# Four modulation halves summed partly by TensorE, their biases added in VectorE's step, and the scores of two heads issued together

## The chip, the cores and the metric

The kernel runs on one core of a Trainium2 chip. The metric is the device time of one execution in microseconds (us), the median of several. The core has five engines that work side by side and wait for one another by semaphores: TensorE (PE: matrix products; PEld is its weight load), VectorE (DVE), ScalarE (ACT), GpSimd (POOL) and SyncE (SP), which issues most of the transfers. Two memories matter here: SBUF, which holds operands, and PSUM, whose eight banks receive the products of TensorE.

## The reference, cut to what matters

One transformer block on a sequence of 512 tokens with 1024 features, all in fp32:

```python
cs = jax.nn.silu(c)
mod = cs @ w_ada + b_ada                       # 1024 -> 6 * 1024
sh1, sc1, g1, sh2, sc2, g2 = split(mod, 6)
h = rmsnorm(x, norm1_g) * (1 + sc1) + sh1
x = x + g1 * mixer(h, ...)                     # 16 heads of three kinds
h = rmsnorm(x, norm2_g) * (1 + sc2) + sh2
x = x + g2 * peer_ffn(h, ...)                  # 8 routed heads over 16384 experts
out = rmsnorm(x, final_g)
```

The mixer projects h by w_in (2560 columns) and has 4 heads of kind A (differential attention: two maps each, over 32 features), 6 of kind B (block attention, which at this length is causal attention over 64 features) and 6 of kind C (sliding window of 128 tokens with a sink, 64 features, two key heads shared by three query heads each). Every head has an ALiBi slope of its own.

## The kernel before, in words

**Start.** SP issues the loads of x, of the first biases, of the first three halves of w_ada (128 partitions x 8 x 512, 2 MB each), then tiles of w_in (w_raw, 0.5 MB each) and the fourth half (lines 825 to 835). `ADA_HALVES` numbers twelve halves of 512 modulation columns; halves 0 to 3 are scale and shift of the first norm. VectorE makes silu(c) and the small lambda and sink values (L1326 to L1338), waiting for ScalarE's exponential in between (L1036); ScalarE squares x (L1039) and takes the root (L1041); VectorE scales x by it (L1345), and TensorE transposes x into the banks (`x_columns`, L416).

**A modulation half** (`mod_half`) is eight VectorE steps over 128x512: L1358 multiplies the first block of w_ada with its silu column, L1360 adds the seven others. The accumulator mod_acc has two places, so half n waits until half n-2 has been used (`half_used`). For halves 0 to 3 TensorE sums over the partitions with one-column products, four per half into one PSUM bank (L427), each followed by a one-row product that adds the bias (L431). `a1_col` and `sh1_col` come out of that bank (L1383, L1385). For halves 4 to 11, `mod_row` on TensorE makes a row on all partitions: one product with ones (L442), one with a single row that adds the bias (L443), and VectorE copies it out (L1373, L1376).

**First normed input.** For each of eight blocks k, ScalarE writes h1_hi (L1071, rounded), VectorE writes h1 (L1390) and subtracts to h1_lo (L1393). `first_two` then projects the first two tiles of w_in with three products per block (L456, L457 and L462); the second of its banks, G, is the one from which the last block of x was read. w_in itself is split in the same way: ScalarE makes w_in_hi (L1048), GpSimd w_in_lo (L956).

**Attention.** It is a list of 64 jobs written out in order, one head on one tile of 128 queries each: kind C for the four query tiles, then A, then B. Iteration J of the loop on TensorE issues, in this order, the scores of job J+2 (L519), pieces of the projections still missing (L475 to L477, L495 to L497), a `mod_row` in some, the transposes of the probabilities of job J (L532), and the product with the values of job J-1 (L552). Score maps alternate between two banks, S0 and S1. VectorE's `soft_in` (L1414) reads a bank, adds the slope times distance, and gives the minimum; ScalarE takes the exponential (L1091) and copies the transposed probabilities (L1099). VectorE's iteration also holds two steps of a modulation half (jobs 0 to 29). In kind B and after it, TensorE transposes the finished output tiles (L563), multiplies by w_out (L578) and transposes the second normed input (L591); VectorE adds the residual (L1482, L1485, L1491) and divides the outputs (`group_out`, L1459). Line L1155 is a root on ScalarE between exponentials, each with a table load.

**The rest,** from about 385 us on, is the routed part: query and key scores, top-16 searches, gates by one-hot products, and a loop over 128 chunks of experts (L672 to L674 and L723), with gathered rows for the first token tile.

The order around the change is the program's own: each engine's list of instructions, the semaphores between them, and SP's single queue. Rows of a head in the array are set by its partitions:

```python
maps = [(h // 2, 2 + h // 2, 64 * (h % 2) + 32 * m, 32) for m in range(2)]     # kind A
[(4 + h // 2, 7 + h // 2, 64 * (h % 2), 64)]                                   # kind B
[(10 + h % CG, 13, 64 * kv, 64)]                                               # kind C, kv = h // CG
```

Of the kernel before, what the change touches and what calls it, by code (L numbers as in the profile page):

```python
# [21 lines left out]
RING = 6  # L22
AHEAD = 8
# [11 lines left out]

def head_plan():


    heads = []
    for h in range(NA):  # L40
        maps = [(h // 2, 2 + h // 2, 64 * (h % 2) + 32 * m, 32) for m in range(2)]
        heads.append(("A", maps, 32 ** -0.5, SLOPES[NCH + h], 256 + h * HD, h * HD, h, h))
    for h in range(NB):
        heads.append(("B", [(4 + h // 2, 7 + h // 2, 64 * (h % 2), 64)], 64 ** -0.5, SLOPES[NCH + NA + h],
                      512 + h * HD if h < 4 else (h - 4) * HD, 256 + h * HD, h, NA + h))
    for h in range(NCH):
        kv = h // CG
        heads.append(("C", [(10 + h % CG, 13, 64 * kv, 64)], 64 ** -0.5, SLOPES[h], 128 + kv * HD,
                      640 + h * HD, h, NA + NB + h))
    return heads  # L50
# [43 lines left out]
def peer_block_kernel(nc, x, c_col, norm1_col, w_ada, b_ada, w_in, w_out, lam_vecs, subln_row, sinks_row,  # L94
# [4 lines left out]
    with ctx:  # L99
# [90 lines left out]
        n1_col = sb("n1_col", [P, KD])  # L190
        a1_col = sb("a1_col", [P, KD])
        sh1_col = sb("sh1_col", [P, KD])
# [3 lines left out]
        subln = sb("subln", [P, HD])  # L196
        sinks = sb("sinks", [P, NCH])
# [37 lines left out]
        s_b, s_n2 = sem("first_biases_loaded"), sem("norm2_loaded")  # L235
        s_ada = [sem(f"ada_loaded{n}") for n in range(4)]
# [127 lines left out]

        def pv_count(J):

            return J + 1 - sum(last <= J for last in LAST)
# [17 lines left out]
        def _(pe):  # L385
# [36 lines left out]
            pe.wait_ge(s_b, 16)  # L422
            for n in range(4):
                pe.wait_ge(s_accd, n + 1)
                for m in range(4):
                    at = n * 4 + m
                    pe.matmul(mcols[:, at:at + 1], mod_acc[:, n % 2, m * P:m * P + P], ones[:, 0:1],  # L427
                              start=True, stop=False)
                    s, b = ADA_HALVES[n]
                    row = s * D + b * 512 + m * P  # L430
                    mm = pe.matmul(mcols[:, at:at + 1], b_first[0:1, row:row + P], ones[0:1, 0:1],  # L431
                                   start=False, stop=True)
                mm.then_inc(full["G"] if n == 3 else s_modu, 1)
            x_columns(KD - 1)

            def mod_row(n):

                b = side["next"]
                ps = take(b, ("row", n))
                pe.wait_ge(s_accd, n + 1)  # L440
                pe.wait_ge(s_bh[n % 3], 16 * ((n - 4) // 3 + 1))
# [69 lines left out]
            def scores(J):  # L511
                i, j = JOBS[J]
                kt = key_tiles(i, j)
                for m, (qt, kk, part, rows) in enumerate(plan[j][1]):
                    s = FIRST_MAP[J] + m
                    ps = take(f"S{s % 2}", ("s", s))
                    for n in NEEDS.get(J, ()):
                        emptied(("qk", n))
                    pe.matmul(ps[:, 0:len(kt) * P], qkT[part:part + rows, qt, i * P:i * P + P],  # L519
                              qkT[part:part + rows, kk, kt[0] * P:(kt[-1] + 1) * P],  # L520
                              start=True, stop=True).then_inc(full[f"S{s % 2}"], 1)
# [277 lines left out]
        def _(sp):  # L799
            def ada(n):  # L800
                s, b = ADA_HALVES[n]
                at = s * D + b * 512
                if n < 4:
                    sp.dma_start(ada_first[n][:, :, :], w_ada[:, at:at + 512].rearrange("(k p) c -> p k c", p=P))\
                      .then_inc(s_ada[n], 16)
                    return
                if n == 4:
                    sp.wait_ge(s_accd, 1)
                elif n == 5:
                    taken(sp, ("xT", KD - 1))  # L810
# [15 lines left out]
            sp.dma_start(b_first[0:1, :], b_ada[0:1, 0:2 * D]).then_inc(s_b, 16)  # L826
            for n in range(3):
                ada(n)
            win(0)
            ada(3)  # L830
# [103 lines left out]
        def _(pool):  # L934
            pool.memset(ident[:, :], 0.0).then_inc(s_const, 1)
# [90 lines left out]
        def _(act):  # L1026
            act.dma_start(c_in[:, :], c_col).then_inc(s_c, 16)
            act.dma_start(n1_col[:, :], norm1_col).then_inc(s_n1, 16)
# [3 lines left out]
            act.dma_start(sinks[:, :], sinks_row.partition_broadcast(P)).then_inc(s_small, 16)  # L1032
            act.wait_ge(s_c, 16)
            act.activation(c_tmp[:, :], c_in[:, :], ACT.Exp, scale=-1.0).then_inc(s_ce, 1)
            act.wait_ge(s_lp, 1)
            act.activation(lam_s[:, 2:4], lam_s[:, 0:2], ACT.Exp).then_inc(s_le, 1)  # L1036
# [4 lines left out]
            act.activation(rstd[:, 0:NT], ss[:, 0:NT], ACT.Sqrt).then_inc(s_std, 1)  # L1041

# [26 lines left out]
            for k in range(KD):  # L1069
                ps = taken(act, ("xT", k))  # L1070
                act.activation(h1_hi[:, k, :], ps[:, :], ACT.Identity, scale=a1_col[:, k:k + 1],  # L1071
                               bias=sh1_col[:, k:k + 1]).then_inc(s_h1hi, 1)
            for n in range(3):
                take_qk(n)
                win_high(n + 3)
# [239 lines left out]
        def _(dve):  # L1315
# [12 lines left out]
            done(dve, dve.tensor_tensor(c_silu[:, :], c_in[:, :], c_tmp[:, :], ALU.mult), s_dv)  # L1328

            dve.wait_ge(s_lam, 16)  # L1330
            done(dve, dve.tensor_tensor(lam_prod[:, :, :], lam_in[:, 0:4:2, :], lam_in[:, 1:4:2, :], ALU.mult), s_dv)
            dve.tensor_reduce(lam_s[:, 0:2], lam_prod[:, :, :], AX, ALU.add).then_inc(s_lp, 1)
            dve.wait_ge(s_le, 1)
            done(dve, dve.tensor_tensor(lam_s[:, 4:5], lam_s[:, 3:4], lam_s[:, 2:3], ALU.subtract), s_dv)
            done(dve, dve.tensor_scalar(lam_s[:, 5:6], lam_s[:, 4:5], -LAM_INIT, None, ALU.add), s_dv)
            dve.wait_ge(s_small, 32)
            done(dve, dve.tensor_scalar(subln[:, :], subln[:, :], 1.0 - LAM_INIT, None, ALU.mult), s_dv)
            done(dve, dve.tensor_scalar(nsinks[:, :], sinks[:, :], -1.0, None, ALU.mult), s_dv)  # L1338

# [3 lines left out]
            done(dve, dve.reciprocal(rstd[:, 0:NT], rstd[:, 0:NT]), s_dv)  # L1343
            for i in range(NT):
                dve.tensor_scalar(x_sb[:, i, :], x_sb[:, i, :], rstd[:, i:i + 1], None, ALU.mult).then_inc(s_xn, 1)  # L1345

            def mod_half(n, first, last):
# [3 lines left out]
                if first == 0:  # L1351
# [31 lines left out]
            done(dve, dve.scalar_tensor_tensor(out=a1_col[:, :], in0=mcols[:, 0:8], scalar=1.0, in1=n1_col[:, :],  # L1383
                                               op0=ALU.add, op1=ALU.mult), s_dv)
            dve.tensor_copy(sh1_col[:, :], mcols[:, 8:16]).then_inc(freeing("mod_cols"), 1)  # L1385
            emptied(dve, "mod_cols")
            for k in range(KD):
                ps = bank[turn[("xT", k)][0]]
                dve.wait_ge(s_h1hi, k + 1)
                dve.tensor_scalar(h1[:, k, :], ps[:, :], a1_col[:, k:k + 1], sh1_col[:, k:k + 1], ALU.mult, ALU.add)\  # L1390
                   .then_inc(freeing(("xT", k)), 1)
                emptied(dve, ("xT", k))
                dve.tensor_tensor(h1_lo[:, k, :], h1[:, k, :], h1_hi[:, k, :].bitcast(f32), ALU.subtract)\  # L1393
                   .then_inc(s_h1lo, 1)
            mod_half(4, 0, KD)
            mod_half(5, 0, KD)
# [107 lines left out]
            for J in range(-2, N + 10):  # L1504
                if J + 2 < N:
                    soft_in(J + 2)
# [338 lines left out]
```

## Time and profile before

| what | value |
|---|---|
| median of 3 runs | 1677.87 us (1677.47 to 1679.64) |
| the profiled execution's own time | 1676.52 us |
| its span, first to last instruction | 1674.7 us |
| mean granted TensorE clock | 0.978 of full speed |
| busy: PE / DVE / ACT / POOL | 1594.0 / 1356.8 / 653.3 / 531.1 us |
| TensorE's clock in 40 slices, tenths | 8799998998999999999999999999999999999999 |
| DMA share in 40 slices, tenths | 9455212001215545656679999999999999999873 |

A slice is 1674.7 / 40 = 41.9 us. Busy time is an average over stages with different limits, so it doesn't say what a change in one stage is worth. The chain of waits does: it starts at the last instruction and goes back, at each step to what released it. "Idle before" beside an instruction is how long its engine stood still, and behind the arrow stands what ended that. The granted clock is 1.00 at 2.4 GHz and 0.50 at 1.2 GHz.

### The profile page before, as it was taken

What the parts mean: (1) busy time and instruction counts of PE and PEld (TensorE: products, weight loads), DVE (VectorE), ACT (ScalarE), POOL (GpSimd) and SP (SyncE); (2) the same over time, 40 slices, a digit from 0 to 9 for tenths busy, and PEclk for the clock granted to TensorE, in tenths of its full rate; (3) what the DMA queues carried; (4) which work ended last, traced back from release to release, by engine and by line L of the source; (5) the groups of instructions that cost most, each with busy time, mean ns of one, the idle gap of its engine ahead of it and who ended that gap; (6) DMA issues with size and microseconds to landing.
All of it is one profiled execution on the core that took longest, in us unless ns stands there. A gap on an engine that the chain in (4) does not pass through costs nothing.

```text
span 1674.7 us, 24817 instructions
## 1 busy us (share of the span) xinstructions
PE 1594.0 (95%) x8451; PEld 1394.1 (83%) x8451; DVE 1356.8 (81%) x2838; ACT 653.3 (39%) x1134; POOL 531.1 (32%) x460
## 2 busy tenths in 40 slices
PE   3799999987999999999999999999999999999997
PEld 2677775547999989998998999999999998888886
DVE  6836752431899999999968988899999998999977
ACT  2234443422323457573753333333333332333332
POOL 2122210013335630001114654545566655222000
PEclk8799998998999999999999999999999999999999
DMA  9455212001215545656679999999999999999873
GB/s 341 149 189 171 92 67 113 25 0 50 77 51 168 164 169 214 207 209 216 240 266 349 390 341 347 341 333 350 379 376 370 370 372 328 378 358 352 274 224 114
DMA packets 162196, 398.79 MB, mean 238 GB/s; under 512 B 11561, under 2 KB 75177, under 8 KB 160433
## 3 DMA queue, kind: packets, MB, share of 16 engines
q1 hardware_dynamic: 114722, 227.06, 39.3%
q0 software_dynamic: 36864, 134.23, 21.7%
q10 hardware_dynamic: 10512, 36.29, 5.6%
q8 instruction: 49, 0.80, 0.2%
q14 instruction: 49, 0.40, 0.1%
HBM read 359.27 MB, written 38.27 MB: 237 GB/s over the span
## 4 chain that ended last, share of the span: by engine, by line
PE 85%; DVE 10%; DMA 2%; ACT 2%; issue 1%; POOL 1%; ACTq 0%; DVEq 0%
PE bank_S L723 15%; PE bank_T L723 10%; PE bank_O L672 5%; PE bank_O L674 5%; PE bank_O L673 5%; PE bank_T L701 5%; PE bank_G L723 5%; PE bank_S L672 4%; PE bank_S L673 4%; PE bank_S L674 4%; PE bank_S L519 2%; PE bank_S L578 2%; PE bank_G L578 2%; PE bank_O L552 2%; PE bank_S L639 2%; DVE mod_acc L1360 2%
## 5 line engine op out<-in xcount | busy, mean ns | idle before, releaser
L1213 ACT ACTIVATE v_hi<-v_raw 128x1024 fp32r<-128x1024 f32 x124 | 131.6, 1062 | 322.1 <-PE bank_G L723 313.7
L1202 ACT ACTIVATE u_hi<-u_raw 128x1024 fp32r<-128x1024 f32 x128 | 135.7, 1061 | 264.7 <-PE bank_O L674 110.1
L1002 POOL COPY stage<-eidx 128x1 uint32<-128x1 uint32 (+1 forms) x128 | 76.5, 598 | 436.2 <-DVE y L1719 184.9
L672 PE MATMUL bank_S<-h_hi,u_hi 128*128 128x384 f32 x512 | 181.0, 354 | 6.3 <-POOL u_lo L989 3.2
L1006 POOL DMA_INDIRECT row<-in_peer_u,stage x128 | 147.5, 1153 | 103.7 <-POOL stage L1002 102.9
L672 PE MATMUL bank_O<-h_hi,u_hi 128*128 128x384 f32 x512 | 171.8, 336 | 0.8 <-DVE u_lo L1755 0.8
L673 PE MATMUL bank_S<-h_lo,u_hi 128*128 128x384 f32 x512 | 172.2, 336 | 0.0
L674 PE MATMUL bank_S<-h_hi,u_lo 128*128 128x384 f32 x512 | 172.2, 336 | 0.0
L674 PE MATMUL bank_O<-h_hi,u_lo 128*128 128x384 f32 x512 | 171.8, 336 | 0.0
L673 PE MATMUL bank_O<-h_lo,u_hi 128*128 128x384 f32 x512 | 171.5, 335 | 0.0
L1719 DVE SCALAR_TENSOR_TENSOR y<-row,wgt,y 128x1024 f32<-128x1024 f32 x128 | 165.9, 1296 | 0.0
L1729 DVE TENSOR_TENSOR v_lo<-v_raw,v_hi 128x1024 fp32r<-128x1024 f32 x124 | 152.0, 1226 | 14.4 <-ACT v_hi L1213 2.9
L1745 DVE SCALAR_TENSOR_TENSOR junk<-row,h 128x1024 f32<-128x1024 f32 x128 | 156.0, 1219 | 0.0
L1006 POOL DMA_INDIRECT row<-in_peer_v,stage x128 | 142.6, 1114 | 41.9 <-issue 29.2
L723 PE MATMUL bank_S<-v_hi,w_hi 128*128 128x512 f32 x372 | 125.3, 391 | 1.5 <-DVE w_lo L1708 1.5
L723 PE MATMUL bank_S<-v_hi,w_lo 128*128 128x512 f32 x372 | 125.4, 391 | 0.0
L723 PE MATMUL bank_S<-v_lo,w_hi 128*128 128x512 f32 x372 | 125.3, 391 | 0.0
L1252 ACT ACTIVATE g_out<-bank_T 128x512 f32<-128x512 f32 x96 | 105.0, 1125 | 49.2 <-PE bank_T L701 40.6
L1676 DVE TENSOR_SCALAR hot_i<-iota_k,cols 128x128 f32<-128x128 f32 x384 | 109.8, 352 | 1.4 <-PE bank_T L701 0.6
L701 PE MATMUL bank_T<-hot_i,hot_j 128*128 128x128 f32 x768 | 101.9, 276 | 4.0 <-DVE hot_j L1678 4.0
L956 POOL TENSOR_TENSOR w_in_lo<-w_raw,w_in_hi 128x1024 fp32r<-128x1024 f32 x20 | 49.3, 2476 | 176.1 <-ACT w_in_hi L1048 176.1
L672 PEld LDWEIGHTS bank_S<-h_hi,u_hi 128*128 128x128 f32 x512 | 97.0, 189 | 9.5 <-issue 9.4
(303 smaller groups left out, 3809.1 us busy)
## 6 DMA issues: line engine op xcount, KB each, us to landing
u_raw<-in_u_t SPq DMA_DIRECT2D x128, 512.0 KB
v_raw<-in_peer_v SPq DMA_DIRECT2D x128, 512.0 KB
gates<-g_out ACTq DMA_DIRECT2D x12, 2048.0 KB, 7.3
g_in<-gates SPq DMA_DIRECT2D x32, 768.0 KB
ada_first<-in_w_ada SPq DMA_DIRECT2D x8, 2048.0 KB, 15.1
spill<-a_act ACTq DMA_DIRECT2D x56, 192.0 KB
a_act<-spill SPq DMA_DIRECT2D x14, 768.0 KB, 10.5
w_raw<-in_w_in SPq DMA_DIRECT2D x20, 512.0 KB, 3.7
```

What stands on the lines that cost most here:

```text
L672: pe.matmul(ps[:, 0:DT], u_hi[:, q, kk], h_hi[:, k, :], start=(k == 0), stop=False)
L673: pe.matmul(ps[:, 0:DT], u_hi[:, q, kk], h_lo[:, k, :], start=False, stop=False)
L674: mm = pe.matmul(ps[:, 0:DT], u_lo[:, q, kk], h_hi[:, k, :], start=False, stop=(k == KD - 1))
L701: mm = pe.matmul(ps[:, tok * P:tok * P + P], hot_j[:, b % 2, tok, :], hot_i[:, b % 2, tok, :], start=True, stop=True)
L723: mm = pe.matmul(y_bank[t][half][:, :], w[:, q, tt], v[:, q, half * 512:half * 512 + 512], start=(first and n == 0), stop=False)
L1006: pool.indirect_dma_start(rows[slot][:, :], None, table[:, :], bass.IndirectOffsetOnAxis(stage[:, place:place + 1], 0))\
L1202: act.activation(u_hi[:, c % 2, :], u_raw[:, c % 2, :], ACT.Copy).then_inc(s_uhi, 1)
L1213: act.activation(v_hi_end[:, i % TAIL, :] if end else v_hi[:, c % 2, :], v_raw[c % 4][:, :], ACT.Copy)\
L1676: dve.tensor_scalar(hot_i[:, B % 2, tok, :], iota_k[:, :], cols[:, 0, n:n + 1], cols[:, 2, n:n + 1], ALU.is_equal, ALU.mult)
L1719: dve.scalar_tensor_tensor(out=y0[:, :], in0=rows[2 * place + 1][:, :], scalar=wgt[:, q], in1=y0[:, :], op0=ALU.mult, op1=ALU.add).then_in ...
L1729: dve.tensor_tensor(lo[:, q, :], v_raw[c % 4][:, :], hi[:, q, :].bitcast(f32), ALU.subtract)\
L1745: dve.scalar_tensor_tensor(out=junk[:, :], in0=rows[2 * place][:, :], scalar=1.0, in1=h2[:, 0, :], op0=ALU.mult, op1=ALU.mult, accum_out=d ...
```

## The change

- Of halves 1, 2 and 3 the first two of eight blocks (`BY_COLUMNS = 2`) are no longer summed by VectorE: TensorE multiplies the 128x128 pieces of w_ada by the silu column directly (`direct`), into 16 more columns of the same bank, 8 products per half. VectorE copies 16 columns, adds the 12 direct ones, and makes a1_col.
- The bias of every half is the addend of VectorE's first step; the one-row products go. For that the bias buffers are 128 partitions, of which GpSimd clears all at its start and a load fills the first. The first biases are loaded on ScalarE's queue behind the clearing.
- x is scaled by ScalarE. The odd blocks of h1 are written by ScalarE as well.
- The lambda values and the sinks' negatives are made later: the lambda products behind the last h1_lo, the rest between halves 4 and 5.
- SP issues the fourth half before the first tile of w_in.
- The heads of kind C change their order in the plan to 0, 3, 1, 4, 2, 5, so that neighbours lie in different halves of the partitions. For kinds B and C, `scores` and `soft_in` take two jobs at once in the iterations in which J + 2 is even, and none in the others.

```diff
+BY_COLUMNS = 2
+C_HEADS = [0, 3, 1, 4, 2, 5]
-    for h in range(NCH):
+    for n, h in enumerate(C_HEADS):
+        def jobs_of(J):
+            if plan[JOBS[J][1]][0] == "A":
+                return [J]
+            return [J, J + 1] if J % 2 == 0 else []
@@ tensor
-            pe.wait_ge(s_b, 16)
-            for n in range(4):
+            pe.wait_ge(s_silu, 1)
+            def direct(n):
+                pe.wait_ge(s_ada[n], 16)
+                for m in range(4):
+                    at = 2 * KD + n * 4 + m
+                    for k in range(BY_COLUMNS):
+                        pe.matmul(mcols[:, at:at + 1], ada_first[n][:, k, m * P:m * P + P], c_silu[:, k:k + 1],
+                                  start=(k == 0), stop=(k == BY_COLUMNS - 1))
+            def columns(n):
                 pe.wait_ge(s_accd, n + 1)
...
-                    mm = pe.matmul(mcols[:, at:at + 1], b_first[0:1, row:row + P], ones[0:1, 0:1],
-                                   start=False, stop=True)
+            direct(1)
+            columns(0)
+            direct(2)
+            columns(1)
+            direct(3)
+            columns(2)
+            columns(3)
...
-                pe.matmul(ps[:, :], ones[:, :], mod_acc[:, n % 2, :], start=True, stop=False)
-                pe.matmul(ps[:, :], ones[0:1, :], b_half[0:1, n % 3, :], start=False, stop=True)\
-                    .then_inc(full[b], 1)
+                pe.matmul(ps[:, :], ones[:, :], mod_acc[:, n % 2, :], start=True, stop=True).then_inc(full[b], 1)
...
+                for a in jobs_of(J):
+                    i, j = JOBS[a]
+                    for m, at in enumerate(plan[j][1]):
+                        n = FIRST_MAP[a] + m
+                        take(f"S{n % 2}", ("s", n))
+                        maps.append((n, at, i, key_tiles(i, j)))
@@ sync
-                if n >= 7:
-                    taken(sp, ("row", n - 3))
+                if n == 4:
+                    sp.wait_ge(s_zero, 2)
-            for n in range(3):
+            for n in range(4):
                 ada(n)
             win(0)
-            ada(3)
@@ gpsimd
+            pool.memset(b_first[:, :], 0.0).then_inc(s_zero, 1)
+            pool.memset(b_half[:, :, :], 0.0).then_inc(s_zero, 1)
@@ scalar
+            act.wait_ge(s_zero, 1)
+            act.dma_start(b_first[0:1, :], b_ada[0:1, 0:2 * D]).then_inc(s_b, 16)
...
+            act.wait_ge(s_rs, 1)
+            for i in range(NT):
+                act.activation(x_sb[:, i, :], x_sb[:, i, :], ACT.Identity, scale=rstd[:, i:i + 1]).then_inc(s_xn, 1)
...
+                if k % 2:
+                    act.activation(h1[:, k, :], ps[:, :], ACT.Identity, scale=a1_col[:, k:k + 1],
+                                   bias=sh1_col[:, k:k + 1]).then_inc(freeing(("xT", k)), 1)
@@ vector
-                    if k == 0:
-                        ins = dve.tensor_scalar(acc, w[:, 0, :], c_silu[:, 0:1], None, ALU.mult)
+                    if k == 0 or k == first and n < 4:
...
+                        ins = dve.scalar_tensor_tensor(out=acc, in0=w[:, k, :], scalar=c_silu[:, k:k + 1], in1=bias,
+                                                       op0=ALU.mult, op1=ALU.add)
...
-            for n in range(4):
-                mod_half(n, 0, KD)
+            mod_half(0, 0, KD)
+            for n in range(1, 4):
+                mod_half(n, BY_COLUMNS, KD)
...
                 if J + 2 < N:
-                    soft_in(J + 2)
+                    for a in jobs_of(J + 2):
+                        soft_in(a)
```

## Rows read from the trace of the kernel before

**Rows 1.** The page, part 4: the chain that ended last, shares by engine.
```profile
PE 85%; DVE 10%; DMA 2%; ACT 2%; issue 1%; POOL 1%; ACTq 0%; DVEq 0%
```

**Rows 2.** Chain of waits, 0 to 125 us: start us, length us, what.
```profile
10.64 4.15 ACT square L1039 x8
...
16.56 2.74 DVE x_sb L1345 x4
...
19.73 0.76 DVE mod_acc L1360
...
29.58 2.72 DVE mod_acc L1360
...
48.87 0.59 PE bank_G L427 x2
...
53.28 0.18 DVE sh_col L1385
...
70.96 1.81 PE bank_S L462 x8
```

**Rows 3.** SP's issues and landings: x, halves 0 and 1, half 3.
```profile
DMA to landing us min/median/max: 8.7/8.7/8.7
...
1.70 10.96 SPq L804 DMA_DIRECT2D ada_first<-in_w_ada  x3
DMA to landing us min/median/max: 14.4/16.9/19.4
...
DMA to landing us min/median/max: 15.8/15.8/15.8
```

**Rows 4.** Timeline, 25 to 66 us: start, length, engine, line, idle before and its end.
```profile
25.36 0.35 PE L427 MATMUL bank_G<-ones,mod_acc 128*128 128x1 f32 x2 [0.40 <-DVE mod_acc L1360]
...
27.50 0.38 PE L431 MATMUL bank_G<-ones,b_first 1*128 1x1 f32 x2
...
36.09 5.49 POOL L956 TENSOR_TENSOR w_in_lo<-w_raw,w_in_hi 128x1024 fp32r<-128x1024 f32 x2 [4.34 <-ACT w_in_hi L1048]
...
53.54 2.12 ACT L1071 ACTIVATE h_hi<-bank_S,sh_col,a_col 128x512 fp32r<-128x512 f32 x3 [16.25 <-DVE sh_col L1385]
...
65.43 0.50 PE L456 MATMUL bank_G<-h_hi,w_in_hi 128*128 128x512 f32 x1 [4.52 <-DVE h L1390]
```

**Rows 5.** Stretches: length, busy PE, PEld, DVE, ACT, POOL; TensorE's clock, DMA share, GB/s.
```profile
30.00:35.00 5.00, 1.87 (x8) 1.83 (x8) 4.89 (x5) 0.05 (x1) 1.74 (x1) 0.50 1.05 398
...
168.00:186.00 18.00, 17.89 (x114) 14.15 (x113) 13.75 (x39) 6.88 (x25) 3.40 (x2) 1.00 0.28 92
...
266.00:272.00 6.00, 6.00 (x21) 4.25 (x22) 1.89 (x8) 2.30 (x9) 0.00 (x0) 0.50 0.34 135
```

**Rows 6.** Chain of waits from 90 us on: start us, length us, what.
```profile
92.53 1.06 PE bank_G L443 x2
...
137.43 0.63 PE bank_S L519 x2
...
225.84 1.06 PE bank_S L519 x4
...
257.36 0.41 PE bank_S L519 x2
...
266.93 1.15 PE bank_S L519 x2
...
302.50 4.29 PE bank_S L578 x10
...
307.67 1.05 PE bank_S L519 x2
...
356.02 6.18 PE bank_S L578 x10
```

**Rows 7.** Timeline of TensorE in kind B, two instructions behind idle time.
```profile
262.72 0.30 PE L532 MATMUL bank_T<-ident,Sb 128*128 128x128 f32 x1 [1.75 <-ACT Sb L1091]
...
299.43 0.66 PE L563 MATMUL bank_S<-ident,o_tile 128*128 128x128 f32 x4 [1.22 <-DVE o_tile L1459]
```

More of the change, by code:

```diff
@@ L426, in _ @@
                     at = n * 4 + m
[L427 to L430, printed above, removed]
-                    mm = pe.matmul(mcols[:, at:at + 1], b_first[0:1, row:row + P], ones[0:1, 0:1],
-                                   start=False, stop=True)
-                mm.then_inc(full["G"] if n == 3 else s_modu, 1)
+                    mm = pe.matmul(mcols[:, at:at + 1], mod_acc[:, n % 2, m * P:m * P + P], ones[:, 0:1],
+                                   start=True, stop=True)
+                mm.then_inc(full["G"] if n == 3 else s_modu, 1)
+            direct(1)
[5 more added lines that the diff above has]
+            columns(3)
             x_columns(KD - 1)
@@ L511, in scores @@
             def scores(J):
[L512 to L517, printed above, removed]
+                maps = []
+                for a in jobs_of(J):
[4 more added lines that the diff above has]
+                        maps.append((n, at, i, key_tiles(i, j)))
+                    for n in NEEDS.get(a, ()):
                         emptied(("qk", n))
-                    pe.matmul(ps[:, 0:len(kt) * P], qkT[part:part + rows, qt, i * P:i * P + P],
+                for n, (qt, kk, part, rows), i, kt in maps:
+                    b = f"S{n % 2}"
+                    pe.matmul(bank[b][:, 0:len(kt) * P], qkT[part:part + rows, qt, i * P:i * P + P],
                               qkT[part:part + rows, kk, kt[0] * P:(kt[-1] + 1) * P],
-                              start=True, stop=True).then_inc(full[f"S{s % 2}"], 1)
+                              start=True, stop=True).then_inc(full[b], 1)
             def transpose_probs(J):
@@ L1327, in _ @@
             done(dve, dve.reciprocal(c_tmp[:, :], c_tmp[:, :]), s_dv)
[L1328 to L1338, printed above, removed]
+            dve.tensor_tensor(c_silu[:, :], c_in[:, :], c_tmp[:, :], ALU.mult).then_inc(s_silu, 1)
+            dve.wait_ge(s_silu, 1)
             dve.wait_ge(s_ss, NT)
@@ L1342, in _ @@
             dve.wait_ge(s_std, 1)
-            done(dve, dve.reciprocal(rstd[:, 0:NT], rstd[:, 0:NT]), s_dv)
-            for i in range(NT):
-                dve.tensor_scalar(x_sb[:, i, :], x_sb[:, i, :], rstd[:, i:i + 1], None, ALU.mult).then_inc(s_xn, 1)
+            dve.reciprocal(rstd[:, 0:NT], rstd[:, 0:NT]).then_inc(s_rs, 1)
             def mod_half(n, first, last):
@@ L1350, in mod_half @@
                 w = ada_first[n] if n < 4 else ada_late[n % 2]
-                if first == 0:
+                if first == 0 or 1 <= n < 4:
                     if n >= 2:
@@ L1377, in mod_row @@
                 ins.then_inc(freeing(("row", n)), 1)
-            for n in range(4):
-                mod_half(n, 0, KD)
+            mod_half(0, 0, KD)
+            for n in range(1, 4):
+                mod_half(n, BY_COLUMNS, KD)
             mcols = taken(dve, "mod_cols")
             dve.wait_ge(s_n1, 16)
-            done(dve, dve.scalar_tensor_tensor(out=a1_col[:, :], in0=mcols[:, 0:8], scalar=1.0, in1=n1_col[:, :],
-                                               op0=ALU.add, op1=ALU.mult), s_dv)
-            dve.tensor_copy(sh1_col[:, :], mcols[:, 8:16]).then_inc(freeing("mod_cols"), 1)
+            done(dve, dve.tensor_copy(m_cols[:, :], mcols[:, 0:2 * KD]), s_dv)
+            done(dve, dve.tensor_tensor(m_cols[:, 4:2 * KD], mcols[:, 2 * KD + 4:4 * KD], m_cols[:, 4:2 * KD], ALU.add),
+                 s_dv)
+            dve.scalar_tensor_tensor(out=a1_col[:, :], in0=m_cols[:, 0:KD], scalar=1.0, in1=n1_col[:, :],
+                                     op0=ALU.add, op1=ALU.mult).then_inc(freeing("mod_cols"), 1)
             emptied(dve, "mod_cols")
@@ L1394, in _ @@
                    .then_inc(s_h1lo, 1)
+            dve.wait_ge(s_lam, 16)
+            done(dve, dve.tensor_tensor(lam_prod[:, :, :], lam_in[:, 0:4:2, :], lam_in[:, 1:4:2, :], ALU.mult), s_dv)
+            dve.tensor_reduce(lam_s[:, 0:2], lam_prod[:, :, :], AX, ALU.add).then_inc(s_lp, 1)
             mod_half(4, 0, KD)
+            dve.wait_ge(s_le, 1)
+            done(dve, dve.tensor_tensor(lam_s[:, 4:5], lam_s[:, 3:4], lam_s[:, 2:3], ALU.subtract), s_dv)
+            done(dve, dve.tensor_scalar(lam_s[:, 5:6], lam_s[:, 4:5], -LAM_INIT, None, ALU.add), s_dv)
+            dve.wait_ge(s_small, 32)
+            done(dve, dve.tensor_scalar(subln[:, :], subln[:, :], 1.0 - LAM_INIT, None, ALU.mult), s_dv)
+            done(dve, dve.tensor_copy(sinks[:, :].rearrange("p (g kv) -> p g kv", g=CG),
+                                      sinks_in[:, :].rearrange("p (kv g) -> p g kv", g=CG)), s_dv)
+            done(dve, dve.tensor_scalar(nsinks[:, :], sinks[:, :], -1.0, None, ALU.mult), s_dv)
             mod_half(5, 0, KD)
```

27 lines of the change are left out of this document (18 added, 9 removed).

## The prediction

> **What bounds the kernel now.** I read the page's chain of waits first: TensorE holds 85% of it [rows 1], so a microsecond taken off TensorE counts wherever TensorE is what is waited for. The change touches only the front of the kernel (up to about 385 us of 1674.7), so I then read that part as a chain in order of time and by stretches. The reader should see three regimes there.
>
> The first 65 us are not TensorE's. VectorE sums the four modulation halves there, in steps of 0.76 us that start every 0.79 us, from 19.3 to 48.8 us; three of the steps take 2.72 us, each beside a GpSimd pass over w_in_lo; then eight one-column products on TensorE, then two small VectorE steps [rows 2]. The second product bank starts only at 65.43, behind VectorE's last h [rows 4].
>
> From 80 to 258 us TensorE has practically no idle time. The stretch 168 to 186 stands for it: TensorE is busy 17.89 of 18 us at the full clock (2.4 GHz), VectorE 13.75 of 18 [rows 5].
>
> From 258 to 385 us TensorE is mostly the bound, with holes: 1.75 us behind the two ScalarE table loads, 1.22 us behind VectorE's o_tile [rows 7].
>
> **Part one, the modulation chain.** x landed 8.7 us after its issue at 0.76, at 9.5 [rows 3], yet the squares ran from 10.64, since the lambda exponential stood ahead of them. That moves away: 1.0 us earlier. The scaling of x goes from VectorE (2.74 for four passes [rows 2]) to ScalarE. Four squares took 4.15 with their reads, so I take four scalings as 4.0: x is ready at 19.5 instead of 19.3, and TensorE's transposes end as now, at about 25.2. No gain there; the gain is that VectorE is free at 15.5.
>
> Half 0 then starts when its weights land, 1.70 + 14.4 = 16.1 [rows 3]. Its first step becomes a 0.76 step, since the bias comes in with it; eight steps at 0.79 make 6.3, to 22.4. Half 1 landed at about 21.5 and has six steps left, 4.7 us, to 27.1. Half 2 needs the accumulator of half 0, and TensorE is late with it: it starts at 25.2 with the eight direct products of half 1, then four columns of half 0. Eight products took 25.36 to 27.88, 0.31 each [rows 4], so twelve take 3.7, to 28.9. VectorE idles 1.8 us, then sums half 2 until 33.6. The next release costs more: the granted clock was 0.50 in all of 30 to 35 (1.2 GHz) [rows 5], after about 3 us in which TensorE had only one-column products or nothing, and eight products took 48.87 to 53.08, 0.52 each [rows 2]. Twelve at 0.52 are 6.2, so columns 1 end at 35.2. Half 3 starts there (its weights, now ahead of w_raw in SP's order, land about 1.3 us before the 17.88 + 15.8 = 33.7 of before [rows 3]).
>
> It starts into GpSimd's passes. The first w_raw takes the old place of half 3 and lands at 33.7; ScalarE needs about 1.1 for it (a square's price), and GpSimd makes three passes, two in a row being 5.49 [rows 4]: 34.8 to about 42.6. Each catches one VectorE step, which then takes 2.72 for 0.76 [rows 2], 2.0 more. Six steps are 4.7, three passes 5.9, less 0.4 as the first pass has begun: 45.5. TensorE's last four columns take 2.1 (the biases' four are gone), three VectorE steps 0.7: 48.3 instead of 53.46 [rows 2]. **5.1 us earlier.** Had the clock stayed high, half 3 would start at 33.7 and all end 1.5 earlier; had the passes cost nothing, half 3 would be done at 40.
>
> Then ScalarE makes eight h_hi and four h: twelve passes at 0.67 (three took 2.12 [rows 4]) are 8.2, so the second bank is free at 56.6 instead of 65.43 [rows 4], **8.8 us earlier** in all. VectorE, with four h and eight h_lo, is done near 58.4 and not the limit. The second bank's sixteen products ran from there to 70.96, 5.5 us, where eight such took 1.81 just behind [rows 2], so sixteen 3.6: TensorE had idled 4.5 us before [rows 4] and began at the low clock. Now it hardly idles: between nothing and 1.9 us more, and I take half, **9.7** in all.
>
> Hidden: GpSimd's two clearing passes before the constants (TensorE waits until 17 us anyway), the later ScalarE queue (its bias load has until 16 us), the lambda and sinks steps, now beside TensorE's projections, where VectorE idles, and the bias buffers' loads on SP. Uncovered, the clearing and the small steps would cost some 3 and 2 us. The later small loads are queued ahead of the squares on ScalarE: about 2 us late, with the same to spare. SP's weight loads 3 to 5 wait for the fourth half as before and come earlier with it.
>
> **Part two, bias rows.** Eight row halves lose their one-row product, 1.06 us each [rows 6], all on the chain and with TensorE busy to both sides: **8.4 us**. Their price on VectorE is 0.28 more for the first step of a half, where it has spare time.
>
> **Part three, pairs of heads.** Two heads of 64 rows now use different halves of the array, to different banks, in succession. The kernel before has no such pair in B and C, but kind A issues two maps of 32 rows: its four records with 512 columns take 1.06, and the two records of one B head with 512 columns take 1.05 [rows 6]. Two maps for the price of one, so I take half of what L519 costs in B and C.
>
> A page prices it lower. The Trainium skill, "TensorE: Matmul & The Clock Gate", section "Measured speedup vs the span model", gives 3.07 times for four row tiles; read as an efficiency of 0.77, the pairs would by estimate save about 9 instead of 13 us. For the same thing the trace has a duration, and it shows none of that loss.
>
> Kind C: 24 jobs, six of 128 columns (0.41 on TensorE) and eighteen of 256 (0.63) [rows 6]. Nine pairs save 9 x 0.63 = 5.7 and two 0.8; the first pair saves nothing, as TensorE waits for VectorE's first two score tiles, and for 0.3 longer: 6.2. Kind B: the pairs issued ahead of the holes lose part. Of the 128-column pairs two count, 0.8; the pair before the table loads is hidden. Of the 256-column pairs one saves 0.63, two run at the low clock, where a head costs 1.15 [rows 6]; the last of them partly, 0.7: 2.5. Of 384 columns two at 0.84 (halfway between 256 and 512), the third lies beside VectorE's residual work (1.22 hole [rows 7]): 1.7. Of 512 two at 1.05: 2.1. Together 7.1, with C **13.3 us**. Both ends: 3 if the softmax chain takes over, 16 if every pair counts.
>
> Against this, the holes at 299 and 328 grow by 0.84 and 1.05. Behind such a hole ten products took 6.18 from 356.02, instead of 4.29 at 302.50 [rows 6], at the low clock. I add one such fall: 1.7. The fall behind the table loads (0.50 in all of 266 to 272 [rows 5]) costs at least 3 us now and stays.
>
> **The sum.** 9.7 + 8.4 + 13.3 - 1.7 = 29.7. The profiled execution took 1676.5 (span 1674.7), so 1646.8; the median of the runs is 1.4 above it: **1648.2 us**. Behind 385 us nothing changes, and loads and gathers follow their releases, so the gain should reach the end.
>
> **Rivals.** (a) The pairs bring nothing: VectorE and ScalarE set the pace. For it: VectorE is 76% busy in 168 to 186 [rows 5], and steps beside GpSimd take three times as long; so too if the tiles do not overlap. Against it: both tiles are issued a step ahead for the second head, and VectorE idled before nearly every score tile. It gives 1648.2 + 13.3 = 1661.5. Chance 0.15.
> The Trainium skill, "TensorEngine Tiling (Array Packing)", section "PSUM Bottleneck", says that the emptying of PSUM may become the limit once tiles speed TensorE up, which is this rival.
> (b) The clock holds: no fall behind the table loads (at least 3 us, by the stretches at 0.50 about 5) and none at the larger holes (1.7): 6.8 less, 1641.4. The table loads' hole stays, so 0.12.
> (c) The head start goes to TensorE's queue: the direct products delay the releases more than worked out, and half 3 meets a fuller GpSimd; four to six less gained, about 1653. Chance 0.08.
> (d) The far side: thinned by the pairs, TensorE between 103 and 257 us loses its clock. A head of 256 columns then costs 1.15 for 0.63, so a fall costs what work lies in it; over 33 us of full-speed work at the low clock make it slower, some 17 falls like that of 356. At 40 us it gives 1688. TensorE has no idle time there to bring it about: 0.03.
> The forecast keeps 0.62.
>
> **Range.** 1641 to 1658: it takes in (b), (c) and the bounds of the head (5 to 12 us) and of the pairs down to 5; (a) and (d) are left out, 0.18. A measurement of this kernel tells about 0.2%, 3.4 us, from no change. Faster 0.96; same 0.01; slower 0.03, from (d).
>
> **What would show it.** Four ada halves summed by about 45.5 with a hole of 1.8 before the third; a_col at about 48; the first product into bank_G at 56 to 57; no L443-like product of one row; pairs of 64-row score records that start together; TensorE without idle time up to the end of kind A, about 235; larger holes at the first two o_tile transposes. I am wrong if kind C takes as long per job as before, or if the head ends after 51.

## The result, and the profile after

| | before | changed |
|---|---|---|
| median | 1677.67 us (1676.73 to 1679.64) | 1634.62 us (1633.23 to 1637.96) |
| span of the profiled execution | 1674.7 us | 1632.1 us |
| mean granted TensorE clock | 0.978 | 0.984 |

The changed kernel is faster by 43.1 us: ratio 0.9745, 95% interval 0.9727 to 0.9762. The forecast was 1648.2, with 1641 to 1658 as its range. The direction was right and every part paid, but the gain was 43 and not 29.5 us, and the time lies 6.4 us below the range.

First the two lines of the page of the changed kernel: busy times, and the chain that ended last, which answers to [rows 1].

```profile
PE 1559.2 (96%) x8451; PEld 1379.8 (85%) x8451; DVE 1351.3 (83%) x2826; ACT 659.1 (40%) x1142; POOL 532.6 (33%) x462
PE 83%; DVE 9%; DMA 3%; ACT 2%; issue 1%; POOL 1%; SPq 1%; DVEq 0%; ACTq 0%
```

TensorE still holds the chain. DMA has a new share, and the chain of the first 62 us shows where (start, length, what; it answers to [rows 2]):

```profile
12.78 19.64 DMA ada_first<-in_w_ada
32.50 0.76 DVE mod_acc L1391
33.29 0.76 DVE mod_acc L1394
34.08 0.76 DVE mod_acc L1394
34.86 2.91 DVE mod_acc L1394
37.80 2.72 DVE mod_acc L1394
40.54 2.72 DVE mod_acc L1394
43.31 1.88 PE bank_G L451 x8
...
45.63 0.18 DVE a_col L1421
```

The fourth half now waits for its own weights, until 32.42, and for nothing else. Three steps of it run at 0.76 and three beside GpSimd's passes at 2.7 to 2.9: the six steps and their price are those of the forecast. They only began 2.7 us sooner than forecast. The timeline of TensorE and GpSimd there says why (it answers to [rows 4]; L444 are the direct products, L451 the columns):

```profile
24.24 1.84 PE L444 MATMUL bank_G<-c_silu,ada_first 128*128 128x1 f32 x16
...
27.04 3.57 PE L444 MATMUL bank_G<-c_silu,ada_first 128*128 128x1 f32 x16
...
30.48 1.84 PE L451 MATMUL bank_G<-ones,mod_acc 128*128 128x1 f32 x8
...
34.85 7.85 POOL L986 TENSOR_TENSOR w_in_lo<-w_raw,w_in_hi 128x1024 fp32r<-128x1024 f32 x3 [28.24 <-ACT w_in_hi L1081]
```

Each product is two records. Eight direct ones start within 1.7 us (24.24 to 25.95) where I took 2.5, and eight at the low clock within 3.4 us (27.04 to 30.48) where I took 4.1.

How the gain grows through the profile. Each mark is a line of either trace (a_col; the last product of the first two projections; the twelfth half's row; the first output product; the last normed input's transposes; the first product with u_hi; the span), before minus after.

| mark | before | after | gained | forecast |
|---|---|---|---|---|
| a_col made | 53.08 | 45.63 | 7.5 | 5.1 |
| third projection starts | 74.4 | 61.4 | 13.0 | 9.7 |
| modulation row of half 11 | 209.25 | 179.16 | 30.1 | 23.3 |
| first output product | 275.25 | 238.23 | 37.0 | |
| last transposes of h | 385.5 | 346.9 | 38.6 | 29.7 |
| first product with u_hi | 502.0 | 462.0 | 40.0 | 29.7 |
| span | 1674.7 | 1632.1 | 42.6 | 29.7 |

The forecast's 23.3 is 9.7, seven of eight bias rows at 1.06, and kind C's 6.2. So 3.3 us of the surplus arose in the head, some 3.5 in kind C, and the rest later.

### The profile page after: what moved, and what is told of

It is laid out like the page before. It is cut to its first block, busy times and chain, and to the rows that moved or that the text cites. A ratio compares the mean times of both kernels' runs of the same rounds, so it can differ in the third digit from the quotient of the medians.

```text
span 1632.1 us, 24855 instructions
## 1 busy us (share of the span) xinstructions
PE 1559.2 (96%) x8451; PEld 1379.8 (85%) x8451; DVE 1351.3 (83%) x2826; ACT 659.1 (40%) x1142; POOL 532.6 (33%) x462
## 4 chain that ended last, share of the span: by engine, by line
PE 83%; DVE 9%; DMA 3%; ACT 2%; issue 1%; POOL 1%; SPq 1%; DVEq 0%; ACTq 0%
PE bank_S L753 15%; PE bank_T L753 10%; PE bank_O L702 5%; PE bank_O L704 5%; PE bank_O L703 5%; PE bank_T L731 5%; PE bank_G L753 5%; PE bank_S L702 4%; PE bank_S L704 4%; PE bank_S L703 4%; PE bank_S L608 2%; PE bank_G L608 2%; PE bank_S L669 2%; PE bank_O L582 1%; PE bank_S L678 1%; DMA u_raw<-in_u_t 1%
## 5 line engine op out<-in xcount | busy, mean ns | idle before, releaser
L731 PEld LDWEIGHTS bank_T<-hot_i,hot_j 128*128 128x128 f32 x768 | 97.6, 191 | 6.5 <-issue 3.3
```

The lines of the kernel that those rows point to most:

```text
L731: mm = pe.matmul(ps[:, tok * P:tok * P + P], hot_j[:, b % 2, tok, :], hot_i[:, b % 2, tok, :], start=True, stop=True)
```

## The experiments

Three theories could hold the surplus of 13 us. The price theory: the forecast's terms were mis-sized, because work in 64 rows or in one row costs TensorE more than its own records. The clock theory: the falls of the granted clock differ between the two kernels. The head theory: the start gained more and the rest is as forecast. Each kernel below was timed beside the kernel before, whose median in these runs was 1675.5 to 1677.4. The intervals of the ratios are about 0.2% to either side, some 3 us, so for smaller differences I go by the marks in the profiles: up to the third projection kernels with the same head agree within 0.6 us.

### Without the pairs

```diff
-            return [J, J + 1] if J % 2 == 0 else []
+            return [J]
```

> The changed kernel with one head per iteration in all kinds. Forecast's price (half of the scores' own time in kinds B and C): 13 us slower than the changed kernel's 1634.6, so 1648. Theory that each block of 64-row products also costs TensorE about 0.2 us at its entry and exit (0.83 instead of 0.63 per block of 256 columns, by the changed kernel's rows): 17 to 18 us slower, 1652. Theory that the pairs brought nothing and all the surplus is clock and head: 1635 to 1638.

Measured: 1652.29 us (ratio 0.9839, 0.9814 to 0.9863), 17.7 slower than the changed kernel, as the price theory had it. But this kernel also had more low clock, so this alone doesn't say whose the 17.7 are; the pair of runs with filled holes below does.

### Pairs in the same rows

```diff
-C_HEADS = [0, 3, 1, 4, 2, 5]
+C_HEADS = [0, 1, 2, 3, 4, 5]
```
(and the sinks copied in their plain order)

> The changed kernel with kind C's heads in their old order 0 to 5, still issued in pairs, so that two of three pairs of kind C lie in the same 64 rows and only the middle one in different halves. If a pair's gain is that both products run at once: the six pairs of 256 columns cost 0.63 more, the two of 128 columns 0.41, together 4.6 us slower, 1639; score records of such a pair then follow one another. If it is issuing them together that gains (fewer changes between products of 128 and of 64 rows): no difference, 1634.6.

Measured: 1636.96 us, 2.3 slower than the changed kernel; in the profiles 0.4 in the span. Neither number was met, so I read the rows. The chain of waits of this kernel, a pair in the same rows and then a pair in different halves, 256 columns each:

```profile
96.24 1.06 PE bank_S L549 x4
...
101.87 0.63 PE bank_S L549 x4
```

Running at once is worth 1.06 - 0.63 = 0.43, and not the 0.63 that a head alone costs. So 0.2 of the 0.63 are paid once per block, however many heads are in it. Six such pairs and two smaller ones make 3.0 us, of which the marks show 1.5 (row of half 11 at 180.69 instead of 179.16). The other half is covered. In the changed kernel TensorE waits for VectorE in kind C, between 60 and 229 us:

```profile
PE bank_S L549 <- DVE low L1464: 1.5, 2, 1.0
PE bank_G L500 <- DVE g_row L1410: 0.8, 1, 0.8
PE bank_S L500 <- DVE sh_row L1410: 0.6, 1, 0.6
PE bank_S L520 <- DVE a_row L1407: 0.2, 1, 0.2
```

In this one, two of those four waits are gone: 0.8 for g_row and 0.8 for the scores are left. The rival (a) of the forecast exists, at 1.5 us and not at 13.

### The bias row, with one row and with all

```diff
-                pe.matmul(ps[:, :], ones[:, :], mod_acc[:, n % 2, :], start=True, stop=True).then_inc(full[b], 1)
+                pe.matmul(ps[:, :], ones[:, :], mod_acc[:, n % 2, :], start=True, stop=False)
+                pe.matmul(ps[:, :], ones[0:1, :], b_half[0:1, n % 3, :], start=False, stop=True)\
+                    .then_inc(full[b], 1)
```
(VectorE's first step of these halves is the 0.48 one again; in bias_full the slices are `0:P`, so the product takes the 127 cleared rows too)

> The changed kernel with the one-row bias product back in the eight modulation rows. Forecast's price 8 x 1.06 = 8.5 us slower, 1643. With a cost of about 0.1 more around a one-row product (0.96 + 1.05 instead of 0.86 per row half): 9.2, 1644.

> As bias_one_row, but the bias product has all 128 rows (127 of them zeros). If the price is that of a product of 512 columns: 8 x 0.86 = 6.9 us slower than the changed kernel, 1641.5. If changing to one row and back costs on top, this kernel is 1.5 to 2.5 us faster than bias_one_row; if row size does not matter, both are the same.

Measured: 1646.08 and 1642.83 us, 11.5 and 8.2 slower than the changed kernel; in the spans 8.7 and 6.7. The order and the distance are as foreseen. The medians lie 1 to 3 us above the expectations: of the four executions of each kernel two had a mean granted clock of 0.978 to 0.980 instead of 0.983 to 0.984, and took 3.6 to 7.2 us longer than the fastest. One row each in the chain of waits of the first and of the second:

```profile
130.76 0.86 PE bank_S L470 x2
131.62 1.05 PE bank_S L471 x2
```

```profile
129.62 0.86 PE bank_S L470 x2
130.48 0.86 PE bank_S L471 x2
```

The same 512 columns take 0.86 with 128 rows and 1.05 with one, in a kernel that differs in nothing else. A product over fewer rows than its neighbours costs more than the full one. That is the second sign of the price theory.

The whole price of a bias row shows in the chains of the kernel before and of no_pairs_fill (below; no pairs either, and no bias rows), at the same place in kind C:

```profile
118.61 0.86 PE bank_S L442 x2
119.47 1.05 PE bank_S L443 x2
120.52 0.26 PE bank_T L532
...
121.01 0.63 PE bank_S L519 x2
```

```profile
101.87 0.86 PE bank_S L469 x2
102.73 0.11 PE bank_T L569
...
103.06 0.63 PE bank_S L549 x2
```

From the row to the scores it is 2.40 with the bias product and 1.19 without: 1.2 per bias row and not 1.06, since 0.15 are booked on the transpose behind it. In the changed kernel less of it shows (8.3 up to the first product with u_hi), because there TensorE waits 0.8 for VectorE's sh_row and a_row, waits that bias_one_row doesn't have.

### The head, one part at a time

no_direct sets `BY_COLUMNS = 0` and leaves out the addition of the direct columns.

> The changed kernel with BY_COLUMNS = 0: halves 1 to 3 are summed by VectorE alone. Two more steps per half: half 1 to 28.7, half 2 to 35.0, half 3 from there to about 47 with GpSimd's three passes inside; a_col at about 49 instead of 45.6. So 3 to 4 us slower than the changed kernel, 1638. If the head start were given back later: 1635.

Measured: 1638.79 us, 4.2 slower. VectorE's a_col came at 48.98 instead of 45.63, 3.4 later, as worked out: the fourth half started at 34.67 instead of 32.50, when its weights set the start, and had two steps more. The first product with u_hi came 4.9 later.

pool_late holds GpSimd:

```diff
+            pool.wait_ge(s_accd, 4)
             for n in range(len(TILES)):
                 win_low(n)
```

> The changed kernel with GpSimd's first w_in_lo pass waiting until the four halves are summed. Theory that each pass adds 2.0 us to the VectorE step beside it: half 3 takes 4.7 instead of 10.7, a_col at about 39.7, and the passes move beside the writing of h, where ScalarE is the pace: 5 to 6 us faster than the changed kernel, 1629. Rival, that the slow steps come from the transfers that land then: half 3 as long as before, and the start 3 to 6 us slower, since w_in_lo is late.

Measured: 1633.5 us, 1.1 faster than the changed kernel, which is within the noise of the medians; its profile:

```profile
33.30 3.90 DVE L1395 SCALAR_TENSOR_TENSOR mod_acc<-ada_first,c_silu,mod_acc 128x512 f32<-128x512 f32 x5
37.29 6.94 POOL L986 TENSOR_TENSOR w_in_lo<-w_raw,w_in_hi 128x1024 fp32r<-128x1024 f32 x3 [30.68 <-DVE mod_acc L1395]
39.92 2.03 DVE L1422 SCALAR_TENSOR_TENSOR a_col<-m_cols,n_col 128x8 f32<-128x8 f32 x1
```

The mechanism is confirmed: the same transfers land at the same time, yet five steps take 3.90 instead of 9.96, and a_col starts at 39.92 instead of 45.63. (It now takes 2.03 for eight columns, being beside a pass itself.) The third projection starts 3.8 us sooner, the last transposes of h 3.2. But at the last product of the first kind with u_hi, at 826, all of it is gone. The next runs show where.

### Filling TensorE's holes

Idle products (`ident` by `dist`, into the bank that TensorE has just taken and will overwrite) ahead of a wait. They change no result.

```diff
                 ps = take(b, ("pT", J))
+                if J == 44:
+                    fill(ps, 2)
```

> The kernel before with two idle products of 512 columns in the hole behind the two table loads alone. Theory that the clock fell for 10 us because of this hole, at a cost of about 5 us: 1672 to 1673.5. Rival: same as before, 1677.7.

> The changed kernel with idle work for TensorE in its holes: two products of 512 columns in the hole behind the two table loads, two, two and three in the holes before the output transposes, twelve in the 11 us before the last normed input. Theory that the falls of the granted clock from 230 us on follow from these holes: no stretch at 0.50 between 225 and 350 us, the last transposes of h at 0.87 us per eight instead of 1.98, 4 to 6 us faster, 1629 to 1631. Rival, that the holes do not decide the clock: the falls stay, same or 1 us slower.

Measured: fill_before 1673.01 us (ratio 0.9974, 0.9959 to 0.999), and fill_after 1632.2, 2.4 faster than the changed kernel (ratios 0.9729 and 0.9745, whose intervals overlap; the first product with u_hi comes 2.9 sooner). Stretches 255 to 262 and 262 to 275 us, of the kernel before and then of fill_before (columns as in [rows 5]):

```profile
255.00:262.00 7.00, 5.75 (x36) 4.19 (x34) 3.86 (x16) 5.27 (x14) 0.00 (x0) 1.00 0.90 324
262.00:275.00 13.00, 12.28 (x44) 8.57 (x45) 5.65 (x20) 6.60 (x23) 0.00 (x0) 0.61 0.47 190
```

```profile
255.00:262.00 7.00, 6.79 (x44) 5.39 (x42) 2.45 (x11) 4.05 (x12) 0.00 (x0) 1.00 0.67 224
262.00:275.00 13.00, 12.96 (x58) 7.82 (x59) 7.03 (x25) 8.71 (x28) 0.00 (x0) 1.00 0.61 245
```

Two idle products in one hole, and 10 us at 1.2 GHz became 2.4 GHz. That hole decided the clock. The five holes of fill_after took away all falls but one, behind the wait for h_lo.

Seven holes filled, in four kernels (the two added fills have three products each, before the first query product's wait for h_hi and h_lo, and before the first product with u_hi):

> The kernel before with idle products in all the holes of TensorE from 255 to 505 us: two behind the table loads, two, two and three before the output transposes, twelve before the last normed input, three before the first query product and three before the first product with u_hi. Its trace has 30.6 us at 0.50 behind 250 us, while TensorE mostly works. Theory that these falls come from the holes: none or one left there, 10 to 12 us faster than before, 1666. Then the rest of the change's 43 us, some 36, is what the changed kernel with the same filling gains over this one. Rival: the falls move elsewhere, 1672 as with one hole filled.

> The changed kernel with the same filling of seven holes. The five of fill_after gave 1632.2 and left one fall behind the wait for h_lo. Theory: that fall goes too, 1 to 2 us faster than fill_after, 1630.5. Rival: idle products there delay the query products, 1632 to 1634.

> As after_fill_all with one head per iteration in all kinds. Without pairs the changed kernel was 17.7 slower, and its trace had 10 us more at 0.50 in kind B. Theory that the pairs themselves give 7 us in kind C and 5 to 6 in kind B, and that the rest came from the clock: 12 to 14 us slower than after_fill_all, 1643 to 1645. Rival, that all 17.7 are the pairs' own: 1648.

> after_fill_all together with GpSimd's passes held until the four halves are summed. In pool_late the first 320 us were 3 to 4 us shorter, and falls of the clock at about 311 and 461 us gave it back. Theory that they fall away with the holes filled: 3.5 us faster than after_fill_all, about 1627. Rival, that something else gave it back: same as after_fill_all.

| kernel | median | span | span, holes unfilled |
|---|---|---|---|
| before_fill_all | 1669.76 | 1667.9 | 1674.7 |
| no_pairs_fill | 1644.88 | 1642.4 | 1650.6 |
| after_fill_all | 1630.51 | 1626.7 | 1632.1 |
| best | 1625.91 | 1623.0 | 1631.8 |

Three of four expectations held. before_fill_all gained 6.8 us in the span and 5.8 in the median (ratio 0.9959, 0.9944 to 0.9974), not 10 to 12: I had counted each low microsecond as half lost. In part of them TensorE was waiting anyway, and idle products may delay the work behind them a little; how much each takes isn't shown. What the granted clock did between 350 and 400 us, in the kernel before and with its holes filled:

```profile
350.00:400.00 50.00, 32.71 (x134) 22.92 (x133) 18.80 (x20) 10.27 (x15) 15.98 (x6) 0.83 0.03 11
```

```profile
350.00:400.00 50.00, 47.03 (x208) 31.78 (x208) 15.73 (x14) 11.49 (x16) 18.59 (x7) 1.00 0.08 22
```

The two spans with filled holes differ by 41.2 us, but that is no price at the full clock: before_fill_all has one fall left, of 3.4 us at 588, in the code that both have, behind a hole of 2.5 us that wasn't filled. Up to the first product with u_hi there is none in either behind the third projection, and the difference there is 494.4 - 457.6 = 36.8, against 40.0 unfilled. So 3.2 of the 40.0 are the clock's. By parts (the first row is before against the kernel without pairs at the third projection, the second the same pair from there to the first product with u_hi, the third the pairs at that product):

| part of the gain | forecast | holes unfilled | holes filled |
|---|---|---|---|
| head | 9.7 | 13.1 | 13.5 |
| bias rows | 8.4 | 9.8 | 9.6 |
| pairs | 13.3 | 17.1 | 13.7 |
| a fall behind a larger hole | -1.7 | in the others | none |
| up to the first product with u_hi | 29.7 | 40.0 | 36.8 |

(In the unfilled 9.8 two differences of the clock nearly cancel: a fall at 103 us that only the kernel before has, and the fall behind the table loads, which is longer in no_pairs, 13.7 us instead of 10.2.)

All of the clock's share is in the row of the pairs. no_pairs and no_pairs_fill between 236 and 252 us:

```profile
236.00:252.00 16.00, 14.05 (x47) 9.40 (x48) 6.87 (x25) 8.46 (x26) 0.00 (x0) 0.57 0.50 200
```

```profile
236.00:252.00 16.00, 15.97 (x64) 8.70 (x64) 6.90 (x25) 8.87 (x28) 0.00 (x0) 1.00 0.49 198
```

At the full clock in both, the pairs are worth 14.4 us in the medians and 15.7 in the spans. Up to the first product with u_hi, behind which the code is the same, they are worth 471.35 - 457.61 = 13.7; unfilled it was 479.09 - 461.98 = 17.1. So 3.4 us of those 17.1 were the clock's. Of the 13.7, kind C has 7.4, by the modulation row of half 11 in after_fill_all and in no_pairs_fill:

```profile
178.93 0.86 PE bank_S L469 x2
```

```profile
186.37 0.86 PE bank_S L469 x2
```

That leaves 6.3 for kind B, where I had forecast 7.1.

`best` is after_fill_all with GpSimd held back: 1625.91 us, ratio 0.971 (0.9687 to 0.9732). It is 4.6 us faster than after_fill_all, where the same wait in the unfilled kernel had brought 1.1. The marks say it more sharply: it is 3.7 ahead at the third projection, at the last transposes of h, at the first product with u_hi and in the span, where pool_late had 3.8, 3.2, 1.7 and 0.3. So what pool_late had given back was the clock's. The stretch 455 to 470 us of pool_late, with nearly the same work as in the changed kernel (0.89 there, 1.00 in the changed one):

```profile
455.00:470.00 15.00, 12.69 (x70) 12.52 (x69) 14.42 (x101) 5.66 (x7) 7.10 (x3) 0.89 0.23 72
```

## Why the prediction was wrong, point by point

The mechanisms were right, but for the clock. At the first product with u_hi the gain was 40.0 and not 29.7. Of the 10.3 us between them about 5.1 are the clock's (1.7 subtracted for a fall, and 3.4 more that it gave), 3.4 the head's, 1.4 the bias rows' and 0.4 the pairs'. Behind that product came 2.6 more. All errors pointed the same way.

- **The head, 3.3 too small.** The failing step is "twelve at 0.52 are 6.2, so columns 1 end at 35.2": they ended at 32.3. The 0.52 and the 0.31 came from rows [rows 2, 4] in which each full column product alternates with a one-row product; products of all rows in succession started 0.21 apart at the full and 0.43 at the low clock. So TensorE was ready for half 3 at about 32.3, and the weights, at 32.42, were the last to come. That gave 2.4 of the 3.3. The rest is the second bank's clock: I took half of 1.9 us, and nearly all of it came, the sixteen products running at 0.23 from the second on. The hidden items were hidden: GpSimd's clearing took 1.80 and 1.37 and nobody waited.
- **Half 3 beside GpSimd's passes** was sized nearly right (35.2 to 45.5, so 10.3, were forecast; 10.8 measured, 32.50 to 43.28, since the first pass had not begun), and pool_late shows the cause.
- **The bias rows, 1.2 to 1.4 too small.** I priced a row by its own record (eight at 1.06 are 8.5, of which the sum took 8.4). It costs 1.2, and the kernel before and the one without pairs differ by 9.6 to 9.8 from the third projection on. bias_one_row gives 8.3 only because the changed kernel has 0.8 of waits in their place.
- **The pairs, 0.4 too small at the full clock and 3.8 with it.** The failing step is "so I take half of what L519 costs in B and C". A pair saves its second stream and also one whole block, and the rows of L519 show only part of what a block costs. The timeline of TensorE in kind C, changed kernel, an iteration with scores and one without:

```profile
121.73 0.61 PE L582 MATMUL bank_O<-v_sb,pT 128*128 128x128 f32 x4
122.27 0.70 PE L549 MATMUL bank_S<-qkT 64*128 64x256 f32 x4
122.90 0.51 PE L500 MATMUL bank_G<-h_hi,w_in_hi 128*128 128x512 f32 x1
123.24 0.40 PE L501 MATMUL bank_G<-h_lo,w_in_hi 128*128 128x512 f32 x1
...
124.64 0.61 PE L582 MATMUL bank_O<-v_sb,pT 128*128 128x128 f32 x4
125.01 0.48 PE L500 MATMUL bank_G<-h_hi,w_in_hi 128*128 128x512 f32 x1
125.32 0.40 PE L501 MATMUL bank_G<-h_lo,w_in_hi 128*128 128x512 f32 x1
```

  From the value products to the second projection product it is 1.51 with a block of scores and 0.68 without: 0.83 per block, not 0.63. The 0.18 before the scores are booked on the line ahead of them. Kind C gave 7.4 instead of 6.2, although TensorE waited there for VectorE more than before. Kind B gave 6.3 instead of 7.1 in spite of the higher price of a block; no run says what took it, so that the sum nearly came out is luck. The Trainium skill, "TensorEngine Tiling (Array Packing)", section "Key Properties", says that changing the tiling mode drains TensorE. The trace agrees in kind: changing to 64-row products and back cost 0.2 us here (0.83 and not 0.63), and a one-row product 0.3 more than one of all rows (1.2 and 0.86). That TensorE drains there, no trace here shows. I cited another section of that page and passed this one over.
- **The lower price for the pairs,** which I had estimated from the Trainium skill, "TensorE: Matmul & The Clock Gate", section "Measured speedup vs the span model" (an efficiency of 0.77), did not come: two heads of 256 columns take 0.63 at once, one takes 0.63. The figure there is for four row tiles, and these are two.
- **The clock, wrong in sign.** The failing step is "I add one such fall: 1.7", with a fall behind the table loads that "stays". The added fall came: a hole grew as forecast, from 1.22 us, with no fall behind it, to 2.02, and 3.4 us at 1.2 GHz followed. But the fall behind the table loads, whose hole is as long as before (1.71 instead of 1.75 us), shrank from 10.2 us to 3.4. The rows are the hole and two stretches of the changed kernel, then one of the kernel before:

```profile
261.46 0.66 PE L593 MATMUL bank_S<-ident,o_tile 128*128 128x128 f32 x4 [2.02 <-DVE o_tile L1509]
231.00:236.00 5.00, 5.00 (x25) 3.64 (x25) 3.69 (x15) 2.97 (x11) 0.00 (x0) 0.66 1.01 401
262.00:266.00 4.00, 3.45 (x17) 2.72 (x15) 2.94 (x5) 3.27 (x9) 0.00 (x0) 0.57 0.57 190
```

```profile
264.00:274.00 10.00, 10.00 (x34) 7.04 (x35) 3.40 (x13) 3.68 (x12) 0.00 (x0) 0.50 0.41 164
```

  And the kernel before had a fall of 3.4 us at 103, behind a hole of 0.4, which the changed one hasn't. It cost about 1.5: from the third projection to the row of half 11 the kernel before took 135.1, and before_fill_all, which has the same code up to there and no such fall in its profile, 133.6. So that fall comes and goes between executions of the same code, and with it part of the surplus is chance. Rival (b), at 0.12, named the direction and gave 1641.4, but its condition, no fall behind the table loads nor behind the larger holes, did not come about. The sizes of the holes don't say where the clock falls: in pool_late no fall followed the same holes of 1.71 and 2.02 us, and one of 3.4 us followed a hole of 1.22. What decides it, no run here shows.
- **Behind 385 us, "nothing changes": 4.0 short.** 1.4 us arose before the loop over keys ended, 2.6 behind the first product with u_hi, in code that is the same in both. In that stretch the kernel before has a fall at 503 us and the changed one has none. From that product to the end the ten profiles without a fall in the loop took 1169.1 to 1171.1 us and the four with one 1171.5 to 1173.5, though the kernels don't differ there. So these 2.6 are not the change's own work.
- **The range.** Its lower end took "16 if every pair counts" as the pairs' bound and let the head's 12 and the clock's 5 stand as alternatives. They were independent, and all three came at once: 12.1 + 8.4 + 16 + 5 would have given 1636, and even that is above the measured 1634.6, since the head and the pairs with their clock passed their own bounds (13.0 and 17.1).

## What to carry to other kernels

Price a short product by the distance between its neighbours with and without it, not by its own record: here one over fewer rows than its neighbours cost 0.2 to 0.3 us more, so group such products, or widen them to all rows. While TensorE is the bound, look at each of its holes of 1 to 3 us for the granted clock behind it. A few idle products in seven holes took away 24 us at half clock here, for 4.4 us up to the first product with u_hi (4.1 by the medians, 1.3 by the ratios to the kernel before, 0.9737 and 0.9745, whose intervals overlap). And measure a small gain with the clock held, or a fall elsewhere can take it or fake it. A GpSimd pass over two tensors beside a chain of VectorE steps cost that chain 2 us each, so start it when the chain is done.

## What the runs showed of the hardware that I had not expected

The granted clock fell while TensorE was busy. Between 25 and 30 us of the changed kernel it was busy 4.94 of 5 us, with one-column products after 24.24, at a mean granted clock of 0.70:

```profile
25.00:30.00 5.00, 4.94 (x32) 4.85 (x32) 4.80 (x7) 0.00 (x0) 0.00 (x0) 0.70 1.05 387
```

Ahead of this fall stands no hole, as there is ahead of the falls from 225 us on: TensorE had transposed x without a break from 19.49 on, and then ran only products of one column. Which of the two matters, or neither, no run here isolates.
